# Layer norm, routing and the first two experts in another order: a fused layer with a mixture of experts on one core

## The reference

```python
def _layer(x, mod, init, ...):
    sh1, sc1, g1, sh2, sc2, g2 = jnp.split(mod, 6, axis=-1)
    y, finals = _mixer(x * (1 + sc1) + sh1, init, ...)
    x = _layer_norm(ALPHA * x + g1 * y, ln1_g, ln1_b)
    f = _moe(x * (1 + sc2) + sh2, w_router, b_router, w_gate, w_up, w_down)
    x = _layer_norm(ALPHA * x + g2 * f, ln2_g, ln2_b)
    return x, finals
# _moe: softmax over 16 experts in 4 groups of 4; the best group by its top 2; the
# top 2 experts in it, their scores normalised; silu(h @ w_gate) * (h @ w_up) @ w_down
```

## Time and profile before

| | us |
|---|---|
| time, median of 3 runs | 816.76 (815.81 to 817.58) |
| the profiled execution | 815.22 |
| its span (first to last instruction) | 813.5 |
| busy: PE 712.0, DVE 578.6, ACT 432.1, POOL 57.8 | |
| chain that ended last, PE's share | 74% |
| TensorE's mean granted clock | 0.94 of 2.4 GHz |

### The profile page before, as it was taken

One profiled execution on the slowest core, in us unless ns is written; L12 is line 12 of the kernel. 1 busy time (PEld: TensorE's weight loads), 2 busy tenths in 40 slices (PEclk: granted clock), 3 DMA queues, 4 the chain that ended last, 5 costly groups with the idle time before them and its releaser, 6 DMA issues.

```text
span 813.5 us, 12342 instructions
## 1 busy us (share of the span) xinstructions
PE 712.0 (88%) x4722; PEld 559.4 (69%) x4722; DVE 578.6 (71%) x834; ACT 432.1 (53%) x596; POOL 57.8 (7%) x90
## 2 busy tenths in 40 slices
PE   2699989899898989999399598999999999999870
PEld 0487978788586978874155486887888888887730
DVE  2559676687685355754554796999999989999765
ACT  1546854254123345660021466888888888888510
POOL 3040000000002000014000020000000000000400
PEclk9699989999999999999779699999999999999995
DMA  9995499899544741239400899999999999998421
GB/s 333 337 326 197 164 341 365 281 395 400 200 173 121 271 165 54 104 37 266 172 0 1 332 411 395 388 396 398 397 398 398 401 401 399 399 397 321 156 80 52
DMA packets 91506, 220.05 MB, mean 271 GB/s; under 512 B 3335, under 2 KB 3631, under 8 KB 91455
## 3 DMA queue, kind: packets, MB, share of 16 engines
q1 hardware_dynamic: 84512, 197.66, 65.4%
q0 software_dynamic: 6528, 21.56, 8.6%
q10 hardware_dynamic: 415, 0.14, 0.1%
HBM read 179.99 MB, written 39.36 MB: 270 GB/s over the span
## 4 chain that ended last, share of the span: by engine, by line
PE 74%; DVE 11%; ACT 6%; DMA 5%; issue 3%; POOL 1%; SPq 0%; DVEq 0%; ACTq 0%; POOLq 0%
PE ps L1128 70%; DMA ring<-in_w_ada 3%; DMA iota<-in_consts 2%; PE ps L1516 2%; ACT w_hi L803 1%; PE ps L1535 1%; DVE arena L1696 1%; DMA arena<-in_b_in 1%; DVE w_lo L1678 0%; ACT arena L913 0%; DVE arena L1827 0%; DVE small L1955 0%; DVE arena L1826 0%; DVE arena L1959 0%; DVE arena L1960 0%
## 5 line engine op out<-in xcount | busy, mean ns | idle before, releaser
L2123 DVE TENSOR_TENSOR w_lo<-arena,w_hi 128x1024 fp32r<-128x1024 f32 x96 | 114.8, 1221 | 15.4 <-ACT w_hi L1027 14.0
L2123 DVE TENSOR_TENSOR w_lo<-ring,w_hi 128x1024 fp32r<-128x1024 f32 x96 | 114.9, 1221 | 8.5 <-ACT w_hi L1027 6.9
L1027 ACT ACTIVATE w_hi<-ring 128x1024 fp32r<-128x1024 f32 x96 | 101.0, 1064 | 17.3 <-PE ps L1128 14.5
L1027 ACT ACTIVATE w_hi<-arena 128x1024 fp32r<-128x1024 f32 x96 | 101.1, 1066 | 15.3 <-PE ps L1128 15.2
L1128 PE MATMUL ps<-h_hi,w_lo 128*128 128x384 f32 x288 | 102.8, 357 | 5.6 <-DVE w_lo L1678 4.4
L1128 PE MATMUL ps<-w_hi,slot_tokens_lo 128*128 128x512 f32 x256 | 103.1, 403 | 4.0 <-DVE w_lo L2123 4.0
L1128 PE MATMUL ps<-w_hi,slot_tokens_hi 128*128 128x512 f32 x256 | 100.8, 394 | 0.0
L1128 PE MATMUL ps<-w_lo,slot_tokens_hi 128*128 128x512 f32 x256 | 100.5, 393 | 0.0
L1128 PE MATMUL ps<-h_hi,w_hi 128*128 128x384 f32 x288 | 98.0, 340 | 0.0
L1128 PE MATMUL ps<-h_lo,w_hi 128*128 128x384 f32 x288 | 97.9, 340 | 0.0
L1678 DVE TENSOR_TENSOR w_lo<-ring,w_hi 128x1024 fp32r<-128x1024 f32 x44 | 53.7, 1225 | 32.9 <-ACT w_hi L803 32.0
(11 more groups left out here) (352 smaller groups left out, 1123.8 us busy)
## 6 DMA issues: line engine op xcount, KB each, us to landing
slot_rows<-arena SPq DMA_DIRECT2D x12, 2048.0 KB, 17.2
ring<-in_w_in SPq DMA_DIRECT2D x11, 2048.0 KB, 12.4
ring<-in_w_ada SPq DMA_DIRECT2D x10, 2048.0 KB, 10.0
ring<-in_w_gate SPq DMA_DIRECT2D x8, 2048.0 KB, 15.1
ring<-in_w_up SPq DMA_DIRECT2D x8, 2048.0 KB, 14.7
ring<-in_w_down SPq DMA_DIRECT2D x8, 2048.0 KB, 11.6
arena<-in_w_gate SPq DMA_DIRECT2D x8, 2048.0 KB
arena<-in_w_down SPq DMA_DIRECT2D x8, 2048.0 KB, 11.3
```

The lines of the kernel that those rows point to most:

```text
L1027: act.activation(w_hi[:, at_ % 4, :], raw[:, q * QUARTER:(q + 1) * QUARTER], ACT.Copy).then_inc(S["hi_ready"], 1)
L2123: tt(w_lo[:, at_ % 4, :], raw[:, q * QUARTER:(q + 1) * QUARTER], w_hi[:, at_ % 4, :].bitcast(F32), ALU.subtract).then_inc(S["lo_dve"], 1)
```

## The change

It has five parts, all in the order of instructions; only the PSUM banks of one gather differ, and one wait is split.

1. **First tile first.** On DVE both halves of tile 0 are mixed into the residual, with their statistics, before the wait for the broadcast rows and the seven passes that fold gain and bias. For that the g1 rows get a semaphore of their own, `g1_in`. The position rows now count on `x2_in`.
2. **The last tile's second pass.** `expert_rows` is cut in two, `centred_rows` and `scaled_rows`. For tile 2 the second comes after `mask` and `chosen`, so `h2_ready` comes there too.
3. **The weights of the two picks** (seven small instructions) come after the routing's row numbers, followed at once by `slots_of(1)`.
4. **Both gathers in a row.** PE does `selected(1)` right after `selected(0)`, into banks 5 and 6, ahead of expert 0's gate product. `tokens_hi` and `tokens_lo` of expert 1 read these banks.
5. **The last expert's slot matrix** is evicted by ACT after expert 1 instead of expert 0. Its transposes on PE stay after expert 0.

DVE's loop over expert pairs starts at pair 1; pair 0 is written out.

```diff
@@ POOL @@
-            modulation([g1_b[:, s, :] for s in range(2)], 0)
+            modulation([g1_b[:, s, :] for s in range(2)], 0, "g1_in")
...
-            pool.dma_start(pos2, a["pos"]...).then_inc(S["pos2_in"], 16)
+            pool.dma_start(pos2, a["pos"]...).then_inc(S["x2_in"], 16)
@@ ACT @@
-            def tokens_hi(n, b):
+            def tokens_hi(n, b, bank=0):
...
-                expert(base, p0, 0, None, False)
+                expert(base, p0, 0, None, False, 0 if base else 5)
+                expert(base + 1, p0, 1, p0 if base else None)
                 if base == 0:
                     last_rows()
-                expert(base + 1, p0, 1, p0 if base else None)
@@ PE @@
                 pe.wait_ge(S["slot_sel"], NT * (b + 1))
-                if b:
-                    pe.wait_ge(S["hg_lo"], 2)
...
-                            last = mm(ps[:, half, k * P:(k + 1) * P], H2[:, i, d0:d0 + P], SEL[b][:, i, :], i == 0, i == NT - 1)
+                            last = mm(ps[:, 5 * b + half, k * P:(k + 1) * P], H2[:, i, d0:d0 + P], SEL[b][:, i, :], i == 0, i == NT - 1)
...
                     selected(0)
+                    selected(1)
                 for q in range(4):
...
-                else:
-                    selected(1)
                 expert(base, 0, p0, True, base > 0)
@@ DVE @@
-            dve.wait_ge(S["x2_in"], 32)
-            dve.wait_ge(S["pos2_in"], 16)
+            dve.wait_ge(S["x2_in"], 48)
             step(tt(X1[:, 1:3, :], X1[:, 1:3, :], pos2, ALU.add))
-            dve.wait_ge(S["ln_in"], 16 * 8)
-            dve.wait_ge(S["g_in"], 16 * 6)
...
+            dve.wait_ge(S["g1_in"], 16 * 2)
...
             mixed_half(0, 1)
-            expert_rows(0)
+
+            dve.wait_ge(S["ln_in"], 16 * 8)
+            dve.wait_ge(S["g_in"], 16 * 4)
+            step(ts(first_row, desc16, -float(P), float(16 * P), ALU.mult, ALU.add))
+            for s in range(2):
+                step(tt(H2[:, 0, :], bias, sc2_b[s], ALU.mult))
+                step(tt(sh2_b[s], sh2_b[s], H2[:, 0, :], ALU.add))
+                step(tt(sc2_b[s], sc2_b[s], gain, ALU.mult))
+            step(ts(bias, bias, ALPHA, None, ALU.mult))
+
+            centred_rows(0)
+            scaled_rows(0)
             for i in range(1, NT):
...
-                expert_rows(i, "h2_ready" if i == NT - 1 else "dve")
+                centred_rows(i)
+                if i < NT - 1:
+                    scaled_rows(i)
...
+            scaled_rows(NT - 1, "h2_ready")
```

More of the change, by code:

```diff
@@ L1057, in out_rows_sb, with expert @@
                     act.activation(OUT[b][:, half * G:(half + 1) * G], ps[:, 5 + half, :], ACT.Copy).then_inc(S["out_sb"], 1)
[L1059 removed]
+            def expert(n, pair, b, stores, before=True, bank=0):
                 up, down, gate = expert_slot(1, b), expert_slot(2, b), expert_slot(0, 1 - b)
@@ L2168, in expert_pass @@
                     last_rows()
-                with dve.Fori(0, NPAIR - 1) as i:
+                expert(base, 0, 0 if base else 5)
+                expert(base + 1, 1)
+                with dve.Fori(1, NPAIR - 1) as i:
                     for b in range(2):
```

44 lines of the change are left out of this document (19 added, 25 removed).

## The result

| | before | after |
|---|---|---|
| time, median, us | 816.28 (815.10 to 817.58, 4 runs) | 791.87 (790.61 to 792.69, 4 runs) |
| profiled execution, and its span | 815.22, 813.5 | 792.69, 790.9 |
| TensorE's mean granted clock | 0.94 | 0.953 |

The ratio is 0.9699 (95%: 0.9678 to 0.9721): 24.4 us off the median, 22.5 off the profiled execution. One execution of a later run (parts 1 and 5) took 3927.81 us and is left out of that run's median.

A forecast was written before the change was run, and what follows sets the result against it. TensorE was taken as the bound, busy 712.0 of 813.5 us, so only its holes pay. 18.0 + 1.3 - 0.5 + 3.7 - 0.3 = 22.2 us off the 816.76 median gave 794.6 us, range 792.8 to 799.0.

The forecast's parts named there:

- Part 1: PE under the projections: the 11.82 us hole, 4.56 in tile 0's transposes and 1.6 behind them go, 18.0 us.
- the 1.6 us of clock: The 24 matmuls between the transposes of tiles 0 and 1: 21.0 us instead of 22.63, a gain of 1.6.
- The margin of DVE: Before tile 1's transposes: DVE meets PE's need at 414.0, PE gets there at 416.7, leaving 2.7 us.
- The rival of the late DVE: DVE becomes the bound under the projections; broadcast rows landing 5 us later cost 2.3, giving 796.9; chance 0.10.
- Part 2: Routing before the first gather: tile 2's second pass leaves the chain, gain 1.3 us, bounds 1.0 and 1.3.
- Part 3: Pick weights behind the row numbers: second slot matrix ready 5.3 us after the first gather began, PE doesn't wait, cost 0.
- Part 4: Expert 0, both gathers in a row: ACT and DVE lose lead, a loss of 0.5 us, bounds 0 and 2.3.
- Part 5: Hole before expert 1's first unit: gain 3.7 us, bounds 0 and 3.9; less 0.3 between experts 1 and 2.
- The second expert: ACT's 1.7 us or the load make an equal hole at the next boundary; 3.4 go, 798.0; chance 0.13.
- Silu: In expert 0, silu holds up the fourth unit and leaves the split chain's 2.3 us open: 796.4; chance 0.04.
- the weights did not run dry: Expert 0's loads end before the later `h2_ready`, delaying expert 1's loads by up to 5.1 us: 799.7; chance 0.06.
- the clock in the loop: Clock falls to 1.2 GHz in the loop, costing up to 18.1 us per expert; with two, 830.8; chance 0.02.

The follow-up runs named there:

- parts 1 and 5: The kernel before with only tile 0 mixed first and the last expert's matrix evicted after expert 1: median 792.05 us, ratio 0.9720.
- the longer fold: The changed kernel with four more DVE passes, 5.0 us in all, between the fold and tile 0's centring: median 799.10 us, ratio 0.9806.
- the gathers apart: The changed kernel with expert 1's gather back behind expert 0's gate product, banks kept: median 792.22 us, ratio 0.9705.
- part 2 undone: The changed kernel with tile 2's second pass back ahead of its router logits: median 790.31 us, ratio 0.9689.
- its up weights brought forward: The changed kernel with expert 1's down piece loaded behind the dispatch wait and expert 1's up piece: median 791.28 us, ratio 0.9708.
- the second measurement of the same kernels: The changed kernel once more, unaltered, with paired times against the kernel before: median 792.66 us, ratio 0.9709.
- part 5 undone: The changed kernel with ACT's eviction of the last expert's matrix back after expert 0: median 798.60 us, ratio 0.9778.

## Why the prediction was off by a little, and where it was right

**Part 1: right.** The hole, the 4.56 us of `turned_rows(0)` and the 1.6 us of clock went as worked out; 18.5 measured for 18.0. Most of the half microsecond (0.3) is in the 24 matmuls between the transposes, 416.96 - 396.28 = 20.7 us where I had taken 21.0. The margin of DVE was 1.2 us and not 2.7, since the broadcast rows landed 1.7 later on the kernel's clock (396.17 against 394.47). The rival of the late DVE was that close. It did not happen, and the run with the longer fold shows what it costs: of 5.0 us added 3.8 lay past the margin, and 8.2 were lost, so the lower clock behind the wait more than doubled the price.

**Part 2: right at its place, worth nothing in the end.** It gave 1.07 of 1.3, since a wait of 0.28 us for PE's sums stayed in front of the copy (the row at 442.32 above). The later `h2_ready` opened no gap in the loads: from 430.6 to 480.0 the DMA share is 1.00. The first step that failed is that the pass "leaves the chain": I followed DVE's chain to the gather and didn't ask what time the transfers would then need. Expert 1's up weights and expert 2's tokens come by a stream that starts with the last projection and not with the gather, and the turn after expert 1 follows that landing by 20.6 us, with part 2 or without. In part 5 I did count it ("the queue of weights starts 1.3 later by this measure") and put expert 1's first unit between 37.5 and 38.8 us after the gather; it came at 482.48, 38.7 after it. That the late end of this range gives back all of part 2 I did not draw from it.

**Part 3: as forecast**, at no cost. **Part 4: the wait is the one forecast.** Expert 1's first gate unit was put at 24.8 us after the gather, with PE asking at 24.2; the row came at 468.41 - 443.75 = 24.7, with PE 0.75 ahead of it. The size of the whole part is another matter: the runs show that it is worth nothing either way. The stretch to the turn lost 1.02 and not 0.5 because of the 0.67 us wait for expert 2's tokens, which is the same stream: with the gathers apart, that wait takes the place of the first (1.59 us), and with part 2 undone the stretch is 36.54, as before the change.

**Part 5: the mis-sized term, and the main step that failed.** Forecast 3.7 and -0.3, together 3.4; measured 4.20 and +0.81, together 5.0. Up to the turn after expert 13 it costs 5.8 when undone and brings 5.1 alone. "The hole is 504.50 - 500.58 = 3.9 us" counted only PE's idle time. For the first hole I had counted what follows it, PE at 1.2 GHz and a second wait of 1.32 us, 6.2 us of the 18.0. For this one I did not look, though the stretches of before shown above have 0.50 from 505 to 507 and 0.70 from 507 to 509. Its timeline of PE there:

```profile
505.28 0.63 PE L1128 MATMUL ps<-w_hi,slot_tokens_hi 128*128 128x512 f32 x1
505.71 0.63 PE L1128 MATMUL ps<-w_hi,slot_tokens_lo 128*128 128x512 f32 x1
...
508.24 0.39 PE L1128 MATMUL ps<-w_hi,slot_tokens_lo 128*128 128x512 f32 x1
508.47 0.39 PE L1128 MATMUL ps<-w_lo,slot_tokens_hi 128*128 128x512 f32 x1
```

From 504.50 the matmuls come every 0.43 us, nine of them, and from 508.24 every 0.23: 9 x 0.2 = 1.8 us. Of that, 0.8 came out in the changed kernel. The rest is held back by expert 1's late loads: with its up weights brought forward, the stretch falls from 18.07 to 17.30, and 18.88 - 17.30 = 1.6 us is close to the whole of it. The 1.7 us of ACT that moved between experts 1 and 2 cost nothing: PE's row at 500.5 has no wait in it.

**Sum.** Over the touched stretch 23.3 for 22.2: 0.5 more from part 1, 1.6 more from part 5, 0.75 less from the parts 2 to 4, in whose place the wait for the stream stands, and 0.2 less in the rest. Off the median it is 24.4, with an interval of 22.8 to 26.3 (0.9678 and 0.9721 of 816.28). The 1.1 us between 23.3 and 24.4 no term explains, and the second measurement of the same kernels has 23.1. My range went 0.8 us beyond the best sum of the terms' bounds, and had nothing for the rest of the program, whose time is not the same in each execution. That is the second fault, and it is no smaller than the first: in 14 profiled executions of 13 kernels that are all alike up to there, "mix" came between 376.73 and 381.67, and the part behind the turn after expert 13 took 71.0 to 73.1.

**The rivals.** The second expert left no hole of ACT's, though its late up weights hold it back as shown above. Silu didn't hold up the fourth unit (PE has no wait between 456.34 and 467.66), the weights did not run dry, and the clock in the loop stayed at 1.00. The Trainium skill's drain of 1.38 us with a table load ("ScalarE: Activation LUTs", section "What ACT_TABLE_LOAD costs") is again not there, on neither side: ACT's copy ahead of the load ends at 461.81 and the load starts at 461.83; it ends at 463.11 and silu starts at 463.13.

The rule on the queues ("DMA: Bandwidth & Descriptors", section "Queues, rings and completion order" of the Trainium skill) got half of its way. The dispatch on POOL's queue landed 10.9 us after its last issue with SP's backlog in full flow, so it did not stand behind it, as the rule says: expert 1's down piece, issued on SP's queue at 442.54, 11.9 us before the dispatch's last issue, landed at 469.1, 3.8 us behind the dispatch. The load that waits for it came no earlier, since it stood behind its own queue.

## What to carry to other kernels

Price a hole together with the work behind it: look at the granted clock of the stretch that follows, each time, even behind 4 us of idle time. When an edit starts something earlier, follow the transfers that the work behind it needs as well: if their stream is full and starts at another event, the gain ends there. To see it, measure from the landing: here that distance repeated to 0.04 us in eight executions, while the one from the gather moved by 1 us. Cut both traces at the same instructions and compare the stretches; the span carries the noise of all that lies before the change.

## What the runs showed of the chip beyond that

**Where the spread comes from.** The largest difference between the executions arises in one stage of the mixer, ahead of everything that was changed. There PE waits 2.41 us for DVE in all of them; here are that row and the stretch around it, in the run with the shortest and in one with nearly the latest "mix" (376.73 and 381.50):

```profile
221.12 1.03 PE L1129 MATMUL ps<-arena 128*32 128x32 f32 x96 [2.41 <-DVE arena L1827]
```

```profile
215.00:235.00 20.00, 16.34 (x210) 12.15 (x209) 14.32 (x20) 4.68 (x6) 0.00 (x0) 0.91 0.60 210
```

```profile
222.10 1.51 PE L1128 MATMUL ps<-arena 128*32 128x32 f32 x96 [2.41 <-DVE arena L1825]
```

```profile
215.00:235.00 20.00, 16.34 (x157) 12.16 (x156) 13.31 (x18) 3.63 (x5) 0.00 (x0) 0.74 0.53 184
```

The wait is the same to the hundredth, the clock behind it is not. It isn't the only source: this row starts between 221.12 and 223.17 in the 14 executions, and from it to "mix" they take 155.6 to 159.4 us. Over 215 to 255 us the mean granted clock has three values in the 14 executions: 0.91 (eight of them, "mix" at 376.7 to 379.9), 0.87 (four, 379.7 to 381.2) and 0.80 (two, 381.5 and 381.7). So whether a short wait is followed by a stretch at 1.2 GHz, and for how long, can differ between executions of the same instructions; why was not tried.

**How long the half clock lasts behind a hole** differs too: in the kernel before it ends near 508, 3.7 us after the matmul at 504.50 behind a wait of 3.95; with part 5 undone near 493, 5.4 us after the matmul at 487.59, behind a wait of the same 3.95. There the stretch to the next turn is 1.0 us longer (19.83 against 18.88).

**Two-megabyte pieces on one queue**, with a dispatch of POOL's between them, kept the DMA engines at a share of 1.00 and together moved 381 GB/s for 49.4 us.
